# Five chunks of the SSD heads as phases between the last seven units of the input product

## What is computed

```python
hn = rmsnorm(h, norm_mix_w[l])
proj = hn @ w_in[l]
(q_sb, k_sb, v_sb, z_ssd, x_ssd, b_ssd, c_ssd, dt_ssd,
 q_hg, f_hg, i_hg, g_hg) = jnp.split(proj, split_at, axis=-1)
o_sb = stick_breaking_group(q_sb, k_sb, v_sb, ...)
o_ssd = ssd_group(z_ssd, x_ssd, b_ssd, c_ssd, dt_ssd, ...)
o_hg = hgrn2_group(q_hg, f_hg, i_hg, g_hg, ...)
h = h + jnp.concatenate([o_sb, o_ssd, o_hg], axis=-1) @ w_out[l]
hn = rmsnorm(h, norm_mlp_w[l])
h = h + jnp.square(jax.nn.relu(hn @ w_up[l])) @ w_down[l]
```

```python
acum = jnp.cumsum(a_c, axis=1)
decay = masked_decay(acum[:, :, None, :] - acum[:, None, :, :], causal)
cb = jnp.repeat(jnp.einsum('btgn,bsgn->btsg', c_c, b_c), rep, axis=-1)
y_diag = jnp.einsum('btsh,bshp->bthp', cb * decay, x_c)
y_off = jnp.einsum('bthn,bhpn->bthp', c_h, state) * jnp.exp(acum)[..., None]
w_end = jnp.exp(acum[:, -1:, :] - acum)
state = state * jnp.exp(acum[:, -1, :])[:, :, None, None] + jnp.einsum('bshn,bsh,bshp->bhpn', b_h, w_end, x_c)
```

## Time and profile before

| | |
|---|---|
| median of 3 runs | 3987.38 us |
| lowest, highest | 3986.21, 3992.94 us |
| profiled execution | 3987.59 us |
| its span | 3985.8 us |
| granted TensorE clock, mean | 0.953 |
| PE, PEld, DVE, ACT, POOL busy | 92%, 74%, 47%, 31%, 2% |

### The profile page before, as it was taken

How to read it: one execution, slowest core, us unless ns; L and a number is a source line. 1 busy time by engine, 2 the same in 40 slices (tenths; PEclk the granted TensorE clock), 3 DMA queues, 4 the chain that set the end, 5 groups by cost and what they waited for, 6 DMA issues and landing times. The chain is left out here.

```text
span 3985.8 us, 48538 instructions
## 1 busy us (share of the span) xinstructions
PE 3654.7 (92%) x18124; PEld 2951.6 (74%) x18124; DVE 1871.6 (47%) x3573; ACT 1220.7 (31%) x2327; POOL 62.9 (2%) x60
## 2 busy tenths in 40 slices
PE   8999999899999999999875889999634999999999
PEld 6888788677777777777654677788534777787887
DVE  4244244453334444444346345533577657754443
ACT  3233133233333333323212234434222432233222
POOL 0000100000000000000000000000010000000000
PEclk9999999999999999999887999999766999999999
DMA  4222232221111111121132201111211322232223
GB/s 138 97 83 69 69 125 104 71 65 56 55 49 44 44 50 50 48 59 50 27 125 111 64 27 44 57 56 46 66 39 51 99 94 81 82 103 95 96 96 121
DMA packets 163324, 289.65 MB, mean 73 GB/s; under 512 B 40697, under 2 KB 103721, under 8 KB 163041
## 3 DMA queue, kind: packets, MB, share of 16 engines
q1 hardware_dynamic: 151888, 263.56, 20.4%
q0 software_dynamic: 9168, 15.58, 1.3%
q10 hardware_dynamic: 2112, 8.39, 0.6%
HBM read 240.39 MB, written 53.31 MB: 74 GB/s over the span
## 5 line engine op out<-in xcount | busy, mean ns | idle before, releaser
L137 ACT ACTIVATE all_w_hi<-all_w_raw 128x1024 fp32r<-128x1024 f32 x303 | 318.6, 1052 | 588.6 <-PE om_z L152 261.1
L142 DVE TENSOR_TENSOR all_w_lo<-all_w_raw,all_w_hi 128x1024 fp32r<-128x1024 f32 x303 | 370.8, 1224 | 259.5 <-ACT all_w_hi L137 259.0
L902 PE MATMUL da_z<-all_hi,all_w_hi 128*128 128x512 f32 x736 | 306.2, 416 | 4.1 <-DVE all_w_lo L142 4.1
L902 PE MATMUL da_z<-all_hi,all_w_lo 128*128 128x512 f32 x736 | 291.6, 396 | 0.0
L902 PE MATMUL da_z<-all_lo,all_w_hi 128*128 128x512 f32 x736 | 290.1, 394 | 0.0
L858 ACT ACTIVATE at_p<-at_logit,da_pair_max 128x256 f32<-128x256 f32 (+1 forms) x384 | 178.1, 466 | 327.8 <-DVE da_pair_max L1058 327.0
L152 PE MATMUL om_z<-all_hi,all_w_hi 128*128 128x512 f32 x640 | 257.5, 402 | 7.6 <-DVE all_w_lo L142 4.5
L152 PE MATMUL om_z<-all_hi,all_w_lo 128*128 128x512 f32 x640 | 256.1, 400 | 0.0
L152 PE MATMUL om_z<-all_lo,all_w_hi 128*128 128x512 f32 x640 | 253.9, 397 | 0.0
L850 ACT ACTIVATE da_pt<-da_tr 128x512 f32<-128x512 f32 (+1 forms) x192 | 101.1, 526 | 476.9 <-PE da_tr L940 476.8
L152 PE MATMUL pr_g<-all_hi,all_w_hi 128*128 128x344 f32 (+1 forms) x624 | 210.4, 337 | 29.9 <-DVE all_lo L1653 25.4
(11 more groups left out here) (532 smaller groups left out, 7448.9 us busy)
## 6 DMA issues: line engine op xcount, KB each, us to landing
all_w_raw<-in_w_mlp SPq DMA_DIRECT2D x128, 512.0 KB, 3.3
all_w_raw<-in_w_ug SPq DMA_DIRECT2D x48, 512.0 KB, 4.2
all_w_raw<-in_w_qkv SPq DMA_DIRECT2D x48, 512.0 KB, 4.4
all_w_raw<-in_w_in SPq DMA_DIRECT2D x27, 512.0 KB, 3.4
da_w_raw<-in_w_qkv SPq DMA_DIRECT2D x24, 512.0 KB
o_groups<-da_o SPq DMA_DIRECT2D x48, 256.0 KB, 2.9
bo_o<-o_groups SPq DMA_DIRECT2D x24, 512.0 KB, 5.4
all_w_raw<-in_w_v SPq DMA_DIRECT2D x20, 512.0 KB, 4.2
```

Of the source, the lines that this page charges most:

```text
L137: self.nc.scalar.activation(self.hi[b][:, :], self.raw[b][:, :], ACT.Copy).then_inc(self.hi_done[b], 1)
L142: self.nc.vector.tensor_tensor(self.lo[b][:, :], self.raw[b][:, :], self.hi[b][:, :].bitcast(F32), ALU.subtract).then_inc(self.lo_done[b], 1)
L902: last = nc.tensor.matmul(z[h][:, :], wp[u][:, ws], ap[:, kk, cols], start=(kk == 0 and m == 0), stop=(kk == KT - 1 and m == 2))
```

## The change

The stage `ssd` goes. Class `Ssd` (moved up in the file) does chunks 0 to 4 as well, inside `projection_and_sticks`: `drive` first runs all 56 slots with the pieces of units 2 to 19 (`apart = 20`), 45 pieces in 56 slots, and then 35 phases with the 21 pieces of units 20 to 26 between them; phase k comes before the pieces of `in_phase(k)`, 0 or 1 of them. The order of units changes: dt comes seventh, then x (7 to 14), z (15 to 18), hf and hi (19 to 22), hq and hg (23 to 26). dt's tables are made in the pieces of units 7 to 10, straight from the evicted unit. POOL, which had no work in this stage, issues the SSD loads: the first x, B, C tile once all x units are stored, the first z tile once all four z units are.

The SSD's tiles need room: `over_x_tiles` lays them, the sticks' value tiles and dt's rows over x. So x is stored to DRAM (`x_out`, eight stores on SP, each released by its addition) and DVE waits for these stores before it writes there; the SP queue of `gated_recurrence` loads x again in turn 2, 4 MB in one DMA. Further tiles of the SSD lie over the sticks' own (`e`, `sp_`, `wt`, `acc`), its PSUM banks are the sticks' banks. Instead of two banks for the state's and the diagonal part of y it has one, so phase 5 on PE waits until DVE has read the first part (`s_y1`), in the last stage too. The stage's other loads (gains, dt bias) and the zero rows move with it.

```diff
-    units = [U_SQ, U_SK, U_SV, U_SQ + 1, U_SK + 1, U_SV + 1] + list(range(U_X, U_X + 8)) + [U_DT, U_HF, U_HF + 1, U_HI, U_HI + 1,
-             U_HQ, U_HQ + 1, U_HG, U_HG + 1, U_Z, U_Z + 1, U_Z + 2, U_Z + 3]
+    units = [U_SQ, U_SK, U_SV, U_SQ + 1, U_SK + 1, U_SV + 1, U_DT] + list(range(U_X, U_X + 8)) + [U_Z, U_Z + 1, U_Z + 2, U_Z + 3,
+             U_HF, U_HF + 1, U_HI, U_HI + 1, U_HQ, U_HQ + 1, U_HG, U_HG + 1]
     NU = len(units)
+    DT, apart = 6, 20
-    is_x = lambda u: 6 <= u < 14
-    is_raw = lambda u: 14 <= u < 19
-    is_silu = lambda u: 19 <= u < NU
+    is_x = lambda u: 7 <= u < 15
+    is_raw = lambda u: 19 <= u < 23
+    is_silu = lambda u: 15 <= u < 19 or 23 <= u < NU
     gated = lambda u: is_x(u) or is_silu(u)
-    n_gated = lambda u: u - 6 if u < 14 else u - 11
+    n_gated = lambda u: u - 7 if u < 19 else u - 11
-    rest = 3 * NU - first_slot
+    rest = 3 * apart - first_slot
+    n_phases = Ssd.PHASES * FIRST
+    in_phase = lambda k: range(3 * apart + 3 * (NU - apart) * k // n_phases, 3 * apart + 3 * (NU - apart) * (k + 1) // n_phases)
+        vt, rows, sd_tile = over_x
+        dtf, tmp, af = (rows[n] for n in ("dtf", "tmp", "af"))
...
+        sd_tile = dict(sd_tile, seg=[by_unit(e[0]), by_unit(e[1])], x=head(sp_[0]), xdt=head(sp_[1]), xw=head(wt[0]), y=head(wt[1]), yd=head(acc),
+                       ss=small[:, 0:2], lnm=small[:, 2:4], rms=small[:, 4:6])
+        sd = Ssd(st, proj, conv, o_cat, keep, sd_tile, (zb[0], zb[1], ob, pb), cst, 0, FIRST)
...
-        def drive(eng, pre_piece, slot):
+        def drive(eng, piece, slot, phase):
             for p in range(6, first_slot):
-                pre_piece(p)
-            for c in range(N + 6):
+                piece(p)
+            for c in range(N):
                 slot(c)
+            for k in range(n_phases):
+                if k < 6:
+                    slot(N + k)
+                phase(k)
+                for p in in_phase(k):
+                    piece(p)
...
+            for k in range(KT):
+                sp.wait_ge(s_xp, k + 1)
+                sp.dma_start(x_out[:, k, :], x[:, k, :]).then_inc(s_kept, 16)
...
+            for u0, n in ((U_Z, 8), (U_HF, 4)):
+                sp.dma_start(proj[u0:u0 + n].rearrange("u p t -> p u t")[:, :, 0:P - META],
+                             zero[:, :].rearrange("p (a t) -> p a t", a=1).broadcast_to([P, n, P - META])).then_inc(s_zout, 16)
             sp.dma_start(conv.rearrange("u p t -> p u t")[:, :, 0:P - META],
                          zero[:, :].rearrange("p (a t) -> p a t", a=1).broadcast_to([P, 8, P - META])).then_inc(s_zout, 16)
...
-            drive(sp, piece, slot)
+            def phase(k):
+                pass
+            drive(sp, piece, slot, phase)
...
+        @block.gpsimd
+        def _(pool):
+            pool.wait_ge(s_zout, 48)
+            for b in range(2):
+                pool.wait_ge(s_gone[b], 16 * 4)
+            sd.load_x(pool, 0)
+            for b in range(2):
+                pool.wait_ge(s_gone[b], 16 * 6)
+            sd.load_z(pool, 0)
+            sd.pool(pool)
...
+                if (u, j) == (DT + 2, 0):
+                    act.wait_ge(s_sdp, 64)
+                    nc.scalar.activation(par[:, 2:3], par[:, 1:2], ACT.Exp).then_inc(s_dte, 1)
+                    act.wait_ge(s_dt, 2)
+                    nc.scalar.activation(tmp, tmp, ACT.Exp, scale=-1.0).then_inc(s_dte, 1)
+                    act.wait_ge(s_dte, 2)
+                    nc.scalar.activation(tmp, tmp, ACT.Ln, bias=1.0).then_inc(s_dte, 1)
+                if (u, j) == (DT + 4, 0):
+                    act.wait_ge(s_dtc, 5)
+                    for name in ("ecum", "wend", "elast"):
+                        nc.scalar.activation(keep[name], keep["cum" if name == "ecum" else name], ACT.Exp).then_inc(s_dtx, 1)
...
+            def phase(k):
+                sd.act(act, k // Ssd.PHASES, k % Ssd.PHASES)
+            drive(act, piece, slot, phase)
...
+                if (u, j) == (DT + 3, 0):
+                    pe.wait_ge(s_dt, 4)
+                    pe.wait_ge(s_pb, 18)
+                    for n, src in enumerate((dtf, af)):
+                        for c in range(NCH):
+                            last = nc.tensor.transpose(pb[:, (n * NCH + c) * SSD_HEADS:(n * NCH + c + 1) * SSD_HEADS], src[:, c * P:c * P + P],
+                                                       ident[0:SSD_HEADS, 0:SSD_HEADS])
+                    last.then_inc(s_dtt, 1)
+                if (u, j) == (DT + 3, 2):
+                    pe.wait_ge(s_dtc, 2)
+                    flat = keep["a"].rearrange("p c h -> p (c h)")
+                    for n, mat in enumerate((cst["upto"], ones)):
+                        last = nc.tensor.matmul(pb[:, n * NCH * SSD_HEADS:(n + 1) * NCH * SSD_HEADS], mat, flat, start=True, stop=True)
+                    last.then_inc(s_dtm, 1)
...
+            def phase(k):
+                if k == 0:
+                    pe.wait_ge(s_w, N)
+                if k == 1:
+                    pe.wait_ge(s_oc, 2 * SB_HEADS)
+                sd.pe(pe, k // Ssd.PHASES, k % Ssd.PHASES)
+            drive(pe, piece, slot, phase)
...
+                if (u, j) == (DT + 1, 1):
+                    dve.wait_ge(s_kept, 16 * KT)
+                    dve.wait_ge(s_sdp, 64)
+                    dve.wait_ge(s_ev, 3 * u)
+                    nc.vector.memset(dtf[:, 0:P - META], 0.0)
+                    nc.vector.memset(tmp[:, 0:P - META], 0.0)
+                    nc.vector.tensor_scalar(dtf[:, P - META:], ev[DT % 3][0:SSD_HEADS, TAPS - 1:], par[:, 0:1], None, ALU.add).then_inc(s_dt, 1)
+                    dve.wait_ge(s_dt, 1)
+                    nc.vector.scalar_tensor_tensor(tmp[:, P - META:], dtf[:, P - META:], -1.0, dtf[:, P - META:], ALU.mult, ALU.max).then_inc(s_dt, 1)
+                if (u, j) == (DT + 2, 1):
+                    dve.wait_ge(s_dte, 3)
+                    nc.vector.scalar_tensor_tensor(dtf[:, P - META:], dtf[:, P - META:], 0.0, tmp[:, P - META:], ALU.max, ALU.add).then_inc(s_dt, 1)
+                    dve.wait_ge(s_dt, 3)
+                    nc.vector.tensor_scalar(af, dtf, par[:, 2:3], -1.0, ALU.mult, ALU.mult).then_inc(s_dt, 1)
```

Class `Ssd` against its form before:

```diff
-    def load(self, pool, i):
+    def load_x(self, pool, i):
...
+    def load_z(self, pool, i):
...
-            pe.wait_ge(self.s_bc, 3 * i + 3)
             for g in range(2):
...
+            pe.wait_ge(self.s_y1, i + 1)
             for g in range(2):
                 for h in range(GH):
-                    last = nc.tensor.matmul(self.pD[:, g * W + h * HD:g * W + (h + 1) * HD], t["seg"][g][:, h, :], t["xdt"][:, g * GH + h, :],
+                    last = nc.tensor.matmul(self.pO[:, g * W + h * HD:g * W + (h + 1) * HD], t["seg"][g][:, h, :], t["xdt"][:, g * GH + h, :],
```

In `gated_recurrence`:

```diff
             def turn(n, b):
+                if n == 2:
+                    sp.dma_start(x[:, :, :], x_in).then_inc(s_x, 16)
```

More of the change, by code:

```diff
@@ L1362, in projection_and_sticks @@
         kn = [st.sb(f"kn{b}", [P, LM]) for b in range(2)]
-        vt = [st.sb(f"vt{b}", [P, 9, P]) for b in range(2)]
+        vt, rows, sd_tile = over_x
+        dtf, tmp, af = (rows[n] for n in ("dtf", "tmp", "af"))
         e = [st.sb(f"e{b}", [P, HALF]) for b in range(2)]
         sp_ = [st.sb(f"sp{b}", [P, HALF]) for b in range(2)]
+        acc = st.sb("acc", [P, HALF])
+        wt = [st.sb(f"wt{b}", [P, HALF]) for b in range(2)]
+        o = [st.sb(f"o{b}", [P, 4, HD]) for b in range(2)]
         big = over_same_bytes(nc, "pr_big", [P, 4, T])
@@ L1390, in projection_and_sticks @@
         pb = st.ps("pb", [P, HALF])
+        par = st.sb("par_dt", [SSD_HEADS, 3])
+        by_unit = lambda t: t[:, :].rearrange("p (u t) -> p u t", t=P)
+        head = lambda t: t[:, :].rearrange("p (h d) -> p h d", d=HD)
+        small = sd_tile["small"]
+        sd_tile = dict(sd_tile, seg=[by_unit(e[0]), by_unit(e[1])], x=head(sp_[0]), xdt=head(sp_[1]), xw=head(wt[0]), y=head(wt[1]), yd=head(acc),
+                       ss=small[:, 0:2], lnm=small[:, 2:4], rms=small[:, 4:6])
+        sd = Ssd(st, proj, conv, o_cat, keep, sd_tile, (zb[0], zb[1], ob, pb), cst, 0, FIRST)
+        s_kept, s_sdp, s_dt, s_dte, s_dtt, s_dtc, s_dtm, s_dtx = (
+            st.sem(n) for n in ("kept", "ssd_par", "dt_s", "dt_exp", "dt_tr", "dt_chunk", "dt_sum", "dt_cum"))
         begin = (g, [zb[0], zb[1], ob[0]])
@@ L1401, in projection_and_sticks @@
         block = st.block()
-        raw_uses = lambda u: len([x_ for x_ in range(14, 19) if x_ < u and x_ % 3 == u % 3])
+        raw_uses = lambda u: len([x_ for x_ in range(19, 23) if x_ < u and x_ % 3 == u % 3])
         ends = {NS * h + s: 2 * h + qb for h in range(SB_HEADS) for qb, s in enumerate((4, NS - 1))}
         summed = lambda c: len([x_ for x_ in range(c) if steps[x_ % NS][1] > 0])
-        def drive(eng, pre_piece, slot):
+        def drive(eng, piece, slot, phase):
             for p in range(6, first_slot):
-                pre_piece(p)
-            for c in range(N + 6):
```

(25 more changed lines are left out.)

584 lines of the change are left out of this document (185 added, 399 removed).

## The result

The changed kernel took 3997.11 us in the median (3991.01 to 4002.63, 16 runs) against 3987.66 (3985.02 to 3992.94, 16 runs): ratio 1.0024, 95% interval 1.0016 to 1.0032. It is slower by 0.24%, 9.5 us. The forecast was 3973, range 3957 to 3995; the time lies 2 us above the range, and on the other side of the time before.

A forecast was written before the change was run, and what follows sets the result against it. TensorE, busy 92% of the span, was taken as the bound, with the SSD stage a hole. Removed -96.2, sticks -54.8, new stretch +111.3 + 18.2 + 2.4, small terms +4.5 gave -14.6 us: 3973, range 3957 to 3995.

The forecast's parts named there:

- Moved out of the sticks: 21 pieces, -79.8 us, +25.0 us: Stick slots: 21 pieces of 3.8 us leave, eleven slots stay empty and expose 25.0 us of waits; net -54.8 us.
- the z wait: Chunk 0, PE in phase 3: waits 9.6 us for z's finish, store and load, then 2.4 us of cold clock.
- the new stretch: SSD phases with 21 pieces between them: 111.3 us of PE work, 18.2 of waits, 2.4 of cold clock; 131.9 us.
- The bound for the sticks: Sticks, worst case: all of the empty slots' wait and 1 us more per slot, so -44 instead of -54.8 us.
- The slower rival: New stretch: pieces and phases don't overlap, as each DVE eviction holds back the next phase; all exposed 4020; chance 0.12.
- Its half case: New stretch: half of the 47 us of further hand-over waits exposed, whole kernel 3997 us.
- The first rival: New stretch: hand-overs take some 5 to 22 us more than summed, gain gone inside 0.2%; 3985 us, chance 0.18.
- the walk: Five SSD chunks followed step by step for PE's waits between phases: 18.2 us, most hand-overs covered by a piece.
- The rule on GpSimd's loads: z loads moved to GpSimd may be held up during DVE fp32 copies: 4.4 us, total 3977; chance 0.05.
- At nothing: Eight x stores, the 4 MB reload of x (12.2 us) and the loads and stores between phases cost no time.
- Small terms: dt's PE work in the sticks 2 us, unit 25's gate at the end 1.5, the recurrence's first load 1; +4.5 us.
- What would show it wrong: PE waiting for DVE over 3 us in each chunk, or the new stretch's clock falling towards 0.7.

The follow-up runs named there:

- the matmuls that nobody reads: Changed kernel with PE repeating unread k tile matmuls in the eleven stick slots without a piece: 3978.60 us, 0.9974 of the kernel before.
- the kernel without pieces there: Changed kernel with all 66 pieces in the sticks and none between the 35 phases: 3986.48 us, 0.9993 of the kernel before.
- k tiles: Changed kernel with PE's products of the 45 stick pieces cut by k tile and spread evenly over 56 slots: 3961.39 us, 0.9929 of the kernel before.

## Why the prediction was wrong

**The step that failed** is "Moved out of the sticks: 21 pieces, -79.8 us, +25.0 us". Its wait was right in sum: 27.1 us more of standing than before against 25.0. By parts, the eleven waits took 29.9 us, three of them 3.8 to 4.5, and the other slots' waits fell from 8.3 to 5.5. What it left out was the clock behind each wait. The prediction had the row for it (4.56 us of waiting, then a piece of 6.2 instead of 3.8 us) and applied it once, to the z wait, and in the bounds to three waits of the new stretch; for the eleven waits of 1.4 to 2.8 us in the sticks it stood in neither the sum nor the bounds. PE was busy 22.9 us longer there, 16.5 of which the matmuls that nobody reads gave back; in one case a wait of 1.43 us was enough. With the 22.9 us the sum is 3996. The bound for the sticks, all of the 25.0 us of waits and 1 us more per slot, put them at 403 us with dt and was 14 us short as well, as it counted no busy time that grows.

**The new stretch**: right in its overlap, lucky in its number. It was forecast as 131.9 and measured as 131.2, as waits 4.9 us too dear met work 4.2 us too cheap. The slower rival (pieces and phases don't overlap) is refuted by that and by the kernel without pieces there. Its half case, 3997, is the time that was measured, by luck: the loss came from the sticks. The first rival's 3985 is also not what happened: no hand-over took longer than in the walk.

**z**: right in its place and 1.8 us too dear. **The rule on GpSimd's loads**: the z loads issued by GpSimd landed in 3.4 to 5.8 us, median 4.2, against SP's median of 4.9 before, and the wait went when the chain started earlier. The Trainium skill's rule (SBUF — State Buffer, "SBUF: two separate sides") would make loads later that GpSimd issues during a DVE copy of fp32 within SBUF. The trace doesn't test it: the copies of a (0.69 us each, at 2820.6, 2845.8, 2866.8 and 2890.3) all lie outside the time from issue to landing of the z loads (issued at 2797.7, 2810.0, 2833.9, 2856.0 and 2881.8).

**At nothing**: x's stores, its reload (14.2 us, in the recurrence's shadow) and the loads between phases held nobody up. **Small terms**: the 4.5 us were about 3 too dear. The last stage took 2.3 us more with as many PE instructions, and PE's waits there were 0.7 us longer in sum; class `Ssd` changed there too, why it took longer is open, and no kernel was made for it. What keeps 14 to 17 us of waits alive under k tiles in the x units' time was not taken apart by a run.

What would show it wrong was named too narrowly: it looked for a low clock in the new stretch, while it fell in the old one.

## What to carry to other kernels

Work taken out of a full stretch gives back less than its duration where it was the cover of a chain: the chain's wait appears, and then the products behind it may run at half rate. Price both for each hole, and look where the clock falls before where PE waits. If there are fewer pieces than slots, cut the pieces finer rather than leave slots empty; the same number of slots with 3.1 us of cover each ran 30 us faster than with 3.8 us in four of five.
